# Hybrid attention layer: the split of the FFN's weights moved ahead, two scratch copies in parts, sixteen-fold queries and keys stored by residue

## The chip, the cores and the metric

One core of a Trainium2 chip runs the whole layer. The metric is the device time of one execution in microseconds (us).

## What is computed

The reference is one transformer layer in float32 on 2048 tokens of width 1024. `z = rmsnorm(x) @ w_in` gives the queries, keys and values of three mixers: sparse attention (compressed, selected and windowed keys), dilated attention with folds 1, 4 and 16, and sliding-window attention with sinks. Their outputs go through `w_out`, a norm and a residual. Then a convolutional GLU feed-forward (FFN) follows with its own norm and residual. The part that the change touches in the attention is this:

```python
for p, (w, r) in enumerate(((128, 1), (512, 4), (2048, 16))):
    def fold(a):
        return a.reshape(n, T // r, r, H, hd).transpose(0, 2, 1, 3, 4).reshape(n * r, T // r, H, hd)
    o, lse = banded_attention(fold(q[:, :, p])[:, :, :, None], fold(k[:, :, p]), fold(v[:, :, p]), w // r, ...)
```

With r = 16 a head falls into 16 independent sequences, one for each residue of the token number modulo 16, with 128 tokens each. A query tile of 128 tokens sees the 128 keys of its own residue.

## The kernel before, in words

The kernel runs five stages, one after another: `project`, `compress`, `attend`, `mix_out`, `ffn`. Between two stages all engines meet at a barrier, at which each engine first drains its own work. Products of float32 matrices are made in three passes from a rounded high part and a low part (high = value rounded to the matmul's type, low = value minus high).

**project.** `z` is made transposed, in 33 blocks j of 128 rows, with all 2048 tokens as columns in four chunks n of 512. For each block, 4 x 8 x 3 matmuls of 128x512 run (L493). Banks 4 to 7 and 0 to 3 of PSUM take turns, so TensorE starts chunk n of block j when the low part of chunk n of block j-2 has been taken. Around it:

- ScalarE rounds the weight block j+1 (`round_w`, L253) once block j-1 is through, and copies each finished chunk from PSUM to `st_hi` (L294).
- GpSimd (POOL) makes the low part of the weight block (`split_w`, L305).
- VectorE makes the low part of each chunk in `st_lo` (L411).
- SyncE issues the stores of `st_hi` and `st_lo` to the scratch tensors `z_hi`, `z_lo` in HBM, in a queue of program order, and the loads of raw weights.

POOL has a second job in this stage. It splits the FFN's weights, 33 pieces of 1 MB (`split_v`, L320 to L325): it waits for piece j, rounds it, issues the store of the high part to `f_hi`, makes the low part, issues the store to `f_lo`, and issues the load of piece j+1 (L312). Before all of it, POOL issues two copies from HBM to HBM of 4 MB each: `w1` to `w1_copy` (read by `compress`) and `w_out` to `wo_copy` (read at the end of `attend`), L337 and L338. The order is written out by hand:

```python
            load_v(0)
            pool.dma_start(w1_copy, w1).then_inc(w1_moved, 16)
            pool.dma_start(wo_copy, w_out).then_inc(wo_moved, 16)
            for j in range(NZ):
                if j >= 1 and j + 2 < NZ:
                    split_w(j + 2)
                split_v(j)
```

At the end of the stage POOL waits until all its stores have landed (L345 and the two lines before it), then drains.

**compress.** It reads the window inputs (`x_raw`, which lie in `h_hi`) and the weights (`w_raw`, which lie in `h_lo`). ScalarE makes the high parts (L623, L626), VectorE the low parts (L650, L654), then TensorE starts (L601). The second half of the weights is loaded by the first instruction of SyncE in this stage (L67).

**attend.** 36 units of 16 query tiles run in a fixed order: first k0, b0, b1, k1, b2, b3 ... k5, b10, b11, then six c units, then the w and s units. k is the compressed attention, b the dilated one; b8 to b11 are the four sixteen-fold heads. For each tile, TensorE makes the scores in two matmuls, queries x high keys (L1174) and queries x low keys (L1175); VectorE adds the bias table `near` and takes the maximum (L1361); ScalarE takes the exponential (L1282); TensorE turns the weights (L1186) and multiplies them with the values (L1211), then turns the output (L1222). Queries and keys of a head are loaded whole, 64 rows of 2048 tokens, from `z_hi` and `z_lo`. For fold 16, TensorE reads them with a step of 16 elements. SyncE's queue loads for the unit after next as soon as the running unit's scores are through: first queries, then keys, then the `near` table (L1008), later values (L1001).

In the tile names of the trace, `low` is the buffer that holds queries and half of the keys.

Of the kernel before, what the change touches and what calls it, by code (L numbers as in the profile page):

```python
# [6 lines left out]
F32 = mybir.dt.float32  # L7
# [3 lines left out]
ALU = mybir.AluOpType  # L11
AX = mybir.AxisListType

P = 128
# [39 lines left out]
V0 = 20  # L54

# [14 lines left out]
def project(nc, x, g_pre, ident, w_z, w_ffn, pos_t, z_hi, z_lo, z_pair, v_heads, gates, f_hi, f_lo, w1, w1_copy, w_out, wo_copy, wo_moved,  # L70
# [4 lines left out]
    with ExitStack() as ctx:  # L75
# [66 lines left out]

        def turned_through(j, n):

            return 4 * (j - V0) + (4 if fold_of(j) == NT else n + 1)
# [17 lines left out]
        def _(sp):  # L163
# [32 lines left out]
            for j in range(2, NZ):  # L196
# [4 lines left out]
                if j == NZ - 1:  # L201
                    for n in range(4):
                        sp.wait_ge(stored[n], stores_through(j - 1))
                    sp.wait_ge(w1_moved, 16)
                    sp.wait_ge(last_row, 2)
                    load_windows(sp, z_pair, x_raw, x2_in, 0)
                    load_first(sp, w1_copy, w1_raw, w1_in, 0)
                    load_windows(sp, z_pair, x_raw, x2_in, 1)
                for n in range(4):
# [7 lines left out]
                    sp.wait_ge(zlo_done, lowered_through(j, n))  # L217
# [15 lines left out]
        def _(act):  # L233
# [43 lines left out]
            for j in range(2, NZ):  # L277
                if j + 1 < NZ:
                    round_w(j + 1)
                for n in range(4):  # L280
                    if is_value(j - 1):

                        act.wait_ge(v_turned, turned_through(j - 1, n))
                    elif j >= 1:

                        act.wait_ge(stored[n], stores_through(j - 1))
# [3 lines left out]
                    if is_plain(j):  # L290
# [6 lines left out]
        def _(pool):  # L297
# [33 lines left out]

            split_w(0)
# [4 lines left out]
            pool.dma_start(w1_copy, w1).then_inc(w1_moved, 16)  # L337
            pool.dma_start(wo_copy, w_out).then_inc(wo_moved, 16)  # L338
            for j in range(NZ):
                if j >= 1 and j + 2 < NZ:  # L340
                    split_w(j + 2)
                split_v(j)
# [5 lines left out]
        def _(dve):  # L348
# [40 lines left out]
            for j in [*range(2, V0 + NV), NZ - 1]:  # L389
                for n in range(4):  # L390
                    if j >= 1:

                        dve.wait_ge(stored[n], stores_through(j - 1))
                    bank = banks[:, 4 * (j % 2) + n, :]
# [13 lines left out]
                    else:  # L408

                        dve.wait_ge(zhi_done, 4 * j + n + 1)  # L410
                        dve.tensor_tensor(st_lo[:, n, 0:512], bank, st_hi[:, n, :].bitcast(F32),  # L411
                                          ALU.subtract).then_inc(zlo_done, 1)
# [350 lines left out]
def attend(nc, ident, z_hi, z_lo, v_heads, gates, bias_b, bias_c, bias_s, bias_w, own_block, sinks, cmp_bias, pick_bias,  # L763
# [112 lines left out]
    with ExitStack() as ctx:  # L876
# [105 lines left out]
        def _(sp):  # L982
# [60 lines left out]
            for u in range(NU):  # L1043
# [21 lines left out]
                if u == NU - 2:  # L1065
                    sp.wait_ge(wo_moved, 16)
# [72 lines left out]
        def _(pe):  # L1139
# [3 lines left out]
            def scores(n, only):  # L1143
# [14 lines left out]
                query = q2[:, qs, :].rearrange(tok, r=unit.fold, j=P)[:, res, b, :]  # L1158
                upper = query
                if unit.kind == "k":  # L1160
                    hi, lo, start = kc_hi[:, unit.h // R, :], kc_lo[:, unit.h // R, :], 0
                else:
                    hi = k_hi[ks].rearrange("p (l r) -> p r l", r=unit.fold)[:, res, :]
                    lo = k_lo[ks].rearrange("p (l r) -> p r l", r=unit.fold)[:, res, :]
                if unit.chosen:
# [969 lines left out]
```

## Time and profile before

| | |
|---|---|
| runs | 3593.09, 3597.2, 3601.05 us; median 3597.2 us |
| profiled execution | 3595.68 us, its span 3593.9 us |
| TensorE (PE) busy | 3413.3 us, 95% of the span |
| VectorE (DVE) busy | 1412.2 us, 39% |
| ScalarE (ACT) busy | 1164.7 us, 32% |
| GpSimd (POOL) busy | 512.1 us, 14% |

`project` takes 0 to about 825 us of the span, `compress` to 862 us, the k, b and c units of `attend` to about 1276 us; the rest is the other attention units, the mix and the FFN. In the rows, a matmul's time overlaps the next one's: the step from start to start is what one costs, the duration is longer. "PE x [7.0 <-POOL y]" means that PE was idle for 7.0 us before x, and that y of POOL ended the wait. The windows view gives the busy time in each stretch by engine, the granted clock of TensorE as a share of 2.4 GHz, and the busy share of the 16 DMA engines.

### The profile page before, as it was taken

What the parts mean: (1) busy time and instruction counts of PE and PEld (TensorE: products, weight loads), DVE (VectorE), ACT (ScalarE), POOL (GpSimd) and SP (SyncE); (2) the same over time, 40 slices, a digit from 0 to 9 for tenths busy, and PEclk for the clock granted to TensorE, in tenths of its full rate; (3) what the DMA queues carried; (4) which work ended last, traced back from release to release, by engine and by line L of the source; (5) the groups of instructions that cost most, each with busy time, mean ns of one, the idle gap of its engine ahead of it and who ended that gap; (6) DMA issues with size and microseconds to landing.
All of it is one profiled execution on the core that took longest, in us unless ns stands there. A gap on an engine that the chain in (4) does not pass through costs nothing. (4 is left out here: it accounts for less than half of the span.)

```text
span 3593.9 us, 45309 instructions
## 1 busy us (share of the span) xinstructions
PE 3413.3 (95%) x16530; PEld 2720.9 (76%) x16530; DVE 1412.2 (39%) x3874; ACT 1164.7 (32%) x1980; POOL 512.1 (14%) x409
## 2 busy tenths in 40 slices
PE   8999999995898999999989969999999999999997
PEld 6788888875787876666657858887888788878886
DVE  5111101104666776666654434412541154115421
ACT  5111111114655765455433323301331133104310
POOL 1454444441000012221010000000000000000000
PEclk9999999997999999999989989999999999999999
DMA  6987765566968732332127665566556655665553
GB/s 200 324 289 258 258 224 176 203 228 178 218 166 200 170 93 59 96 94 55 51 77 234 199 218 193 193 234 233 192 196 234 228 196 197 234 216 206 196 191 117
DMA packets 297668, 676.17 MB, mean 188 GB/s; under 512 B 98704, under 2 KB 154512, under 8 KB 283408
## 3 DMA queue, kind: packets, MB, share of 16 engines
q1 hardware_dynamic: 265616, 517.93, 45.1%
q0 software_dynamic: 31840, 155.40, 12.1%
q8 instruction: 135, 2.21, 0.3%
q14 instruction: 77, 0.63, 0.1%
HBM read 496.06 MB, written 185.57 MB: 190 GB/s over the span
## 5 line engine op out<-in xcount | busy, mean ns | idle before, releaser
L1855 PE MATMUL f_banks<-low,f_w_hi 128*128 128x512 f32 x2816 | 871.3, 390 | 27.1 <-DMA f_w_lo<-f_lo 19.8
L1855 PEld LDWEIGHTS f_banks<-low,f_w_hi 128*128 128x128 f32 x2816 | 529.8, 188 | 140.4 <-issue 25.4
L1855 PE MATMUL f_banks<-low,f_w_lo 128*128 128x512 f32 x1408 | 548.8, 390 | 0.0
L1211 PE MATMUL a_ot_ps<-a_turned_w,a_vs 128*65 128x256 f32 (+3 forms) x1452 | 448.7, 421 | 1.1 <-issue 1.1
L493 PE MATMUL z_banks<-h_hi,z_w_hi 128*128 128x512 f32 x972 | 388.3, 399 | 7.0 <-POOL z_w_lo L305 7.0
L493 PE MATMUL z_banks<-h_lo,z_w_hi 128*128 128x512 f32 x972 | 385.3, 396 | 0.0
L493 PE MATMUL z_banks<-h_hi,z_w_lo 128*128 128x512 f32 x972 | 385.2, 396 | 0.0
L1855 PEld LDWEIGHTS f_banks<-low,f_w_lo 128*128 128x128 f32 x1408 | 265.0, 188 | 54.5
L1282 ACT ACTIVATE w_small<-w_small,a_negm 128x128 f32<-128x128 f32 (+3 forms) x510 | 249.4, 519 | 173.4 <-DVE a_negm L1361 108.3
L1875 PE MATMUL f_banks<-f_w_hi,f_g_hi 128*128 128x512 f32 x704 | 278.4, 396 | 0.0
L1875 PE MATMUL f_banks<-f_w_hi,f_g_lo 128*128 128x512 f32 x704 | 278.4, 396 | 0.0
L1875 PE MATMUL f_banks<-f_w_lo,f_g_hi 128*128 128x512 f32 x704 | 278.4, 395 | 0.0
L294 ACT ACTIVATE st_hi<-z_banks 128x512 fp32r<-128x512 f32 (+1 forms) x116 | 69.3, 598 | 540.8 <-PE z_banks L493 397.9
L1211 PEld LDWEIGHTS a_ot_ps<-a_turned_w,a_vs 128*65 128x65 f32 x1452 | 179.0, 139 | 82.7 <-issue 70.1
L1361 DVE CUSTOM_DVE_ANT_0 w_small<-a_s_ps,near 128x128 f32<-128x128 f32 (+2 forms) x456 | 170.5, 394 | 168.7 <-PE a_s_ps L1175 139.6
L493 PEld LDWEIGHTS z_banks<-h_hi,z_w_hi 128*128 128x128 f32 x972 | 183.5, 189 | 50.1 <-POOL z_w_lo L305 7.4
L493 PEld LDWEIGHTS z_banks<-h_lo,z_w_hi 128*128 128x128 f32 x972 | 183.2, 188 | 44.4
L493 PEld LDWEIGHTS z_banks<-h_hi,z_w_lo 128*128 128x128 f32 x972 | 183.3, 189 | 42.7
L1959 DVE SCALAR_TENSOR_TENSOR f_y<-f_banks,vk,f_gp 128x1024 f32<-128x1024 f32 x16 | 20.5, 1284 | 494.7 <-POOL vk L1808 494.2
L411 DVE TENSOR_TENSOR st_lo<-z_banks,st_hi 128x512 fp32r<-128x512 f32 x76 | 52.6, 692 | 406.2 <-ACT st_hi L294 406.2
L1186 PE MATMUL a_t_ps<-a_idt,w_small 128*128 128x128 f32 x1092 | 212.1, 277 | 0.0
L1268 ACT ACTIVATE a_turned_w<-a_t_ps 128x512 f32<-128x512 f32 (+3 forms) x255 | 138.7, 549 | 198.9 <-PE a_t_ps L1186 198.0
(212 smaller groups left out, 5302.3 us busy)
## 6 DMA issues: line engine op xcount, KB each, us to landing
f_w_hi<-f_hi SPq DMA_DIRECT2D x264, 512.0 KB, 3.5
f_w_lo<-f_lo SPq DMA_DIRECT2D x264, 512.0 KB, 4.5
z_xs<-in_w_ffn POOLq DMA_DIRECT2D x33, 1024.0 KB, 8.6
f_hi<-z_v_hi POOLq DMA_DIRECT2D x33, 1024.0 KB, 4.9
f_lo<-z_xs POOLq DMA_DIRECT2D x33, 1024.0 KB, 6.4
low<-z_hi SPq DMA_DIRECT2D x48, 512.0 KB, 7.7
z_hi<-st_hi SPq DMA_DIRECT2D x84, 256.0 KB, 4.5
z_lo<-st_lo SPq DMA_DIRECT2D x84, 256.0 KB, 5.1
```

What stands on the lines that cost most here:

```text
L294: act.activation(out.bitcast(F32) if is_value(j) else out, bank, ACT.Copy).then_inc(zhi_done, 1)
L411: dve.tensor_tensor(st_lo[:, n, 0:512], bank, st_hi[:, n, :].bitcast(F32), ALU.subtract).then_inc(zlo_done, 1)
L493: last = pe.matmul(banks[:, 4 * k + n, :], w[:, k, c, :], h[:, c, tok], start=(c == 0 and q == 0), stop=(c == DC - 1 and q == 2))
L1186: ins = pe.transpose(t_ps[:, b % TB, i, :], weights(n)[:, x * P:(x + 1) * P], idt[:])
L1211: last = pe.matmul(ot_ps[0:out_width(g), at:at + count * P], values, rows, start=(x == 0), stop=(x == len(blocks) - 1), skip_group_check=True)
L1268: ins = eng.activation(out, src, ACT.Copy) if e == 0 else eng.tensor_copy(out, src)
L1282: act.activation(weights(n), weights(n), ACT.Exp, bias=negm[:, n % 32:n % 32 + 1], scale=-1.0)\
L1361: dve.tensor_tensor_reduce(weights(n)[:, a:z], s_ps[:, c % SB, 0:z - a], table[:, at + a:at + z], -0.125, floor, ALU.add, ALU.min, low).th ...
L1855: last = pe.matmul(banks[:, bank, :], w[:, s % RING, c * P:(c + 1) * P], h[:, c, :], start=(c == 0 and x == 0), stop=(c == DC - 1 and x == 2))
L1875: last = pe.matmul(banks[:, 2 * t + n, :], g[:, d, tok], w[:, s % RING, cols], start=(d == 0 and x == 0), stop=(d == NF - 1 and x == 2))
L1959: dve.scalar_tensor_tensor(out=y[:], in0=banks[:, 2 * t:2 * t + 2, :].rearrange("p b n -> p (b n)"), scalar=rstd[:, t:t + 1], in1=gp[:], o ...
```

## The change

1. **The FFN split.** Its loop starts at j = 1, with `split_w(3)` ahead of `split_v(0)`, and at j = 4, 8 and 12 it does two pieces. So the last piece is done at j = 30, with the last `split_w`.
2. **The copies.** `w1` and `w_out` are moved in 16 parts of 256 KB each, one of either after the split at j = 6 to 21.
3. **By residue.** For the blocks 7, 8 (queries b8 to b11) and 18, 19 (their keys), the copies from PSUM to `st_hi` and `st_lo` put the 128 tokens of each residue next to each other. A chunk of 512 tokens then goes to all four slots of the buffer, so ScalarE and VectorE wait for all four stores of the block before, and SyncE stores a chunk only after all four have been lowered. In `attend`, queries and keys of fold 16 are read as 128 neighbouring columns.

```diff
+RESIDUE_BLOCKS = (7, 8, 18, 19)
+TWICE = (4, 8, 12)
+MOVES = tuple(range(6, 22))
...
+        def by_residue(bank):
+
+            return bank.rearrange("p (l m a) -> p m a l", m=4, a=4)
+
+        def residues(tile, n):
+
+            return tile[:, :, 0:512].rearrange("p m (a l) -> p m a l", a=4)[:, :, :, n * P // 4:(n + 1) * P // 4]
...
-                    sp.wait_ge(w1_moved, 16)
+                    sp.wait_ge(w1_moved, 16 * len(MOVES))
...
-                    sp.wait_ge(zlo_done, lowered_through(j, n))
+                    sp.wait_ge(zlo_done, lowered_through(j, 3 if j in RESIDUE_BLOCKS else n))
...
+                    elif j in RESIDUE_BLOCKS and n == 0:
+                        for m in range(4):
+                            act.wait_ge(stored[m], stores_through(j - 1))
...
-                    if is_plain(j):
+                    if j in RESIDUE_BLOCKS:
+                        act.activation(residues(st_hi, n), by_residue(bank), ACT.Copy).then_inc(zhi_done, 1)
+                    elif is_plain(j):
...
+            def move(i):
+
+                m, c = divmod(i, len(MOVES) // 2)
+                rows = slice(c * (CMP * HD * 2 // len(MOVES)), (c + 1) * (CMP * HD * 2 // len(MOVES)))
+                pool.dma_start(w1_copy[m, rows], w1[m, rows]).then_inc(w1_moved, 16)
+                rows = slice(i * (D // len(MOVES)), (i + 1) * (D // len(MOVES)))
+                pool.dma_start(wo_copy[rows], w_out[rows]).then_inc(wo_moved, 16)
...
-            pool.dma_start(w1_copy, w1).then_inc(w1_moved, 16)
-            pool.dma_start(wo_copy, w_out).then_inc(wo_moved, 16)
-            for j in range(NZ):
-                if j >= 1 and j + 2 < NZ:
+            v = 0
+            for j in range(1, NZ):
+                if j + 2 < NZ:
                     split_w(j + 2)
-                split_v(j)
+                for _ in range(2 if j in TWICE else 1):
+                    if v < NZ:
+                        split_v(v)
+                        v += 1
+                if j in MOVES:
+                    move(MOVES.index(j))
...
+                    if j in RESIDUE_BLOCKS and n == 0:
+                        for m in range(1, 4):
+                            dve.wait_ge(stored[m], stores_through(j - 1))
...
-                        dve.tensor_tensor(st_lo[:, n, 0:512], bank, st_hi[:, n, :].bitcast(F32),
-                                          ALU.subtract).then_inc(zlo_done, 1)
+                        low, high = st_lo[:, n, 0:512], st_hi[:, n, :].bitcast(F32)
+                        if j in RESIDUE_BLOCKS:
+                            low, high, bank = residues(st_lo, n), residues(st_hi.bitcast(F32), n), by_residue(bank)
+                        dve.tensor_tensor(low, bank, high, ALU.subtract).then_inc(zlo_done, 1)
...
-                    sp.wait_ge(wo_moved, 16)
+                    sp.wait_ge(wo_moved, 16 * len(MOVES))
...
+                if unit.fold == NT:
+                    query = q2[:, qs, res * P:(res + 1) * P]
...
+                    if unit.fold == NT:
+                        hi, lo = (k[:, res * P:(res + 1) * P] for k in (k_hi[ks], k_lo[ks]))
```

The queue of POOL at the start of the FFN split, before (z_w_lo is the low part of a weight block, z_v_hi and z_xs the two parts of an FFN piece):

```order
L305 TENSOR_TENSOR z_w_lo<-z_w_raw,z_w_hi 128x1024 x3
L312 DMA z_xs<-in_w_ffn 128x2048
L337 DMA w_copy<-in_w 64x16384
L338 DMA wo_copy<-in_w_out 64x16384
L320 TENSOR_SCALAR z_v_hi<-z_xs 128x2048
L322 DMA f_hi<-z_v_hi 128x2x1024
L323 TENSOR_TENSOR z_xs<-z_xs,z_v_hi 128x2048
L325 DMA f_lo<-z_xs 128x2x1024
L312 DMA z_xs<-in_w_ffn 128x2048
L305 TENSOR_TENSOR z_w_lo<-z_w_raw,z_w_hi 128x1024
```

The same place of POOL's queue now:

```order
L321 TENSOR_TENSOR z_w_lo<-z_w_raw,z_w_hi 128x1024 x3
L328 DMA z_xs<-in_w_ffn 128x2048
L321 TENSOR_TENSOR z_w_lo<-z_w_raw,z_w_hi 128x1024
L336 TENSOR_SCALAR z_v_hi<-z_xs 128x2048
L338 DMA f_hi<-z_v_hi 128x2x1024
L339 TENSOR_TENSOR z_xs<-z_xs,z_v_hi 128x2048
L341 DMA f_lo<-z_xs 128x2x1024
L328 DMA z_xs<-in_w_ffn 128x2048
L321 TENSOR_TENSOR z_w_lo<-z_w_raw,z_w_hi 128x1024
```

The two large copies are gone from here, and weight block 3 is lowered ahead of the first FFN piece.

The end of POOL's queue in `project`, before, from the last weight block on (L75 is the barrier, L580 is the next stage):

```order
L305 TENSOR_TENSOR z_w_lo<-z_w_raw,z_w_hi 128x1024
L320 TENSOR_SCALAR z_v_hi<-z_xs 128x2048
L322 DMA f_hi<-z_v_hi 128x2x1024
L323 TENSOR_TENSOR z_xs<-z_xs,z_v_hi 128x2048
L325 DMA f_lo<-z_xs 128x2x1024
L312 DMA z_xs<-in_w_ffn 128x2048
...
L323 TENSOR_TENSOR z_xs<-z_xs,z_v_hi 128x2048
L325 DMA f_lo<-z_xs 128x2x1024
L75 UNCONDITIONAL_BRANCH
```

The same place now (L78 is the barrier):

```order
L321 TENSOR_TENSOR z_w_lo<-z_w_raw,z_w_hi 128x1024
L336 TENSOR_SCALAR z_v_hi<-z_xs 128x2048
L338 DMA f_hi<-z_v_hi 128x2x1024
L339 TENSOR_TENSOR z_xs<-z_xs,z_v_hi 128x2048
L341 DMA f_lo<-z_xs 128x2x1024
L78 UNCONDITIONAL_BRANCH
```

Before, three pieces of the FFN came after the last weight block, now one. The two-piece rounds stand between weight blocks 6 and 7, 10 and 11, 14 and 15.

## Rows read from the trace of the kernel before

**Rows 1.** Who TensorE waited for, 0 to 1250 us: in total, times, longest.
```profile
PE c_hid L601 <- DVE h_lo L654: 29.0, 1, 29.0
PE z_banks L493 <- POOL z_w_lo L305: 7.0, 1, 7.0
```

**Rows 2.** Timeline of POOL, 78 to 135 us: start, duration, engine, line, operation.
```profile
81.56 0.54 POOL L337 DMA_DIRECT2D w_copy<-in_w  x1
...
95.25 0.57 POOL L312 DMA_DIRECT2D z_xs<-in_w_ffn  x1
...
122.60 1.91 POOL L320 TENSOR_SCALAR z_v_hi<-z_xs 128x2048 fp32r<-128x2048 f32 x1 [24.36 <-DMA z_xs<-in_w_ffn]
```

**Rows 3.** Windows behind that wait: stretch, length, busy PE PEld DVE ACT POOL, PEclk, DMA share.
```profile
134.20:139.50 5.30, 5.30 (x13) 4.14 (x14) 0.00 (x0) 0.00 (x0) 0.00 (x0) 0.50 1.01 373
139.50:150.00 10.50, 10.50 (x46) 8.46 (x45) 1.38 (x2) 1.20 (x2) 7.04 (x3) 1.00 0.58 227
```

**Rows 4.** Timeline of POOL, one later round of the FFN split.
```profile
272.99 2.40 POOL L305 TENSOR_TENSOR z_w_lo<-z_w_raw,z_w_hi 128x1024 fp32r<-128x1024 f32 x1 [10.78 <-ACT z_w_hi L253]
...
284.05 0.57 POOL L312 DMA_DIRECT2D z_xs<-in_w_ffn  x1
295.39 2.40 POOL L305 TENSOR_TENSOR z_w_lo<-z_w_raw,z_w_hi 128x1024 fp32r<-128x1024 f32 x1 [10.78 <-ACT z_w_hi L253]
```

**Rows 5.** Timelines of POOL, SyncE's queue and PE around the end of `project`.
```profile
805.33 1.89 POOL L320 TENSOR_SCALAR z_v_hi<-z_xs 128x2048 fp32r<-128x2048 f32 x1 [11.18 <-DMA z_xs<-in_w_ffn]
...
813.11 0.75 POOL L325 DMA_DIRECT2D f_lo<-z_xs  x1 [0.30 <-POOL z_xs L323]
825.37 0.31 POOL L580 MEMSET kc_hi<- 128x256 f32 x1 [11.51 <-POOLq L75]
...
806.38 0.43 SPq L230 DMA_DIRECT2D z_lo<-st_lo  x1
...
833.16 0.56 PE L601 MATMUL c_hid<-c_x_hi,h_hi 128*128 128x260 f32 x1 [29.05 <-DVE h_lo L654]
```

**Rows 6.** Timelines of DVE and POOL around the next barrier.
```profile
861.51 0.29 DVE L675 COPY vk<-c_vc_ps 127x128 f32<-127x128 f32 x1 [0.17 <-PE c_vc_ps L614]
...
862.60 1.80 POOL L1086 MEMSET k_lo<- 64x2048 f32 x1 [36.31 <-POOLq L518]
```

**Rows 7.** The instruction group of ScalarE that reads with a step of eight elements.
```profile
L623 ACT ACTIVATE c_x_hi<-h_hi 128x1024 fp32r<-128x1024 f32 x4 | 8.1, 2080 | 0.0
```

**Rows 8.** SyncE's two loads of `w1_copy` (L67), its line's view.
```profile
DMA to landing us min/median/max: 8.6/13.0/17.4
```

**Rows 9.** Timeline of PE, scores of unit k0, then of unit b8.
```profile
880.68 0.27 PE L1174 MATMUL a_s_ps<-kc_hi,low 128*128 128x128 f32 x1
880.79 0.28 PE L1175 MATMUL a_s_ps<-kc_lo,low 128*128 128x128 f32 x1
...
1090.24 0.39 PE L1174 MATMUL a_s_ps<-k_hi,low 128*128 128x128 f32 x1
1090.46 0.39 PE L1175 MATMUL a_s_ps<-k_lo,low 128*128 128x128 f32 x1
```

**Rows 10.** Windows of the units b8, b9, k5, b10, b11; columns as in rows 3.
```profile
1087.10:1102.00 14.90, 14.13 (x87) 12.59 (x86) 10.41 (x56) 9.41 (x24) 0.00 (x0) 1.00 0.69 180
1102.00:1115.20 13.20, 13.20 (x98) 13.20 (x98) 8.61 (x43) 9.83 (x23) 0.00 (x0) 1.00 0.91 200
1115.20:1127.10 11.90, 10.58 (x86) 9.03 (x85) 8.04 (x46) 7.93 (x22) 0.00 (x0) 1.00 1.05 272
1127.10:1150.30 23.20, 17.35 (x90) 14.72 (x89) 12.47 (x71) 8.69 (x23) 0.30 (x1) 0.78 0.59 147
1150.30:1166.80 16.50, 15.08 (x112) 14.35 (x110) 13.12 (x88) 10.65 (x27) 1.69 (x4) 1.00 0.97 246
```

**Rows 11.** Timeline of DVE at the first tiles of k5 and b10.
```profile
1117.09 0.29 DVE L1361 CUSTOM_DVE_ANT_0 w_small<-a_s_ps,near 128x128 f32<-128x128 f32 x1 [1.31 <-DMA near<-in_cmp_bias]
...
1132.67 0.29 DVE L1361 CUSTOM_DVE_ANT_0 w_small<-a_s_ps,near 128x128 f32<-128x128 f32 x1 [4.91 <-DMA near<-in_bias_b]
```

## The prediction

> **What bounds the kernel now.** I read the waits of TensorE first, because the page has it busy for 95% of the span: whatever does not shorten its matmuls or its waits is worth nothing. Up to the c units it has two waits that the moved work of POOL could touch [rows 1]: 29.0 us before the first product of `compress`, and 7.0 us before a product of `project`. The rest of `project` runs without a gap, one weight block of 96 matmuls every 22.4 us (start to start of the low parts in [rows 4]).
>
> The timeline of POOL explains the 7.0 us. At 81.56 it issues the 4 MB copy of `w1`, and right behind it the one of `w_out` [rows 2]. The load of FFN piece 1, issued at 95.25, meets these copies in the DMA engines, and POOL waits 24.36 us for it, until 122.60. Only after that piece's round of 9.2 us (275.39 to 284.62 in [rows 4]) comes `split_w(4)`, and TensorE, which was through at 127.2, starts block 4 at 134.2. Its clock was granted at 0.5 until 139.5, that is 1.2 instead of 2.4 GHz [rows 3]: twelve matmuls took 5.3 us, while later 45 took 10.5 us, 0.233 us each.
>
> The end of `project` explains the 29.0 us [rows 5]. TensorE ends at 833.16 - 29.05 = 804.1, SyncE issues its last store until 806.8. POOL still waits for piece 32 until 805.33, splits it, issues the store of its low part until 813.9, waits for that to land and drains. The next stage begins at 825.4. Where POOL is not last, a barrier costs 0.8 us (last work ends at 861.8, first starts at 862.6 [rows 6]).
>
> For the sixteen-fold heads I compared score matmuls of one shape. In k0, where queries and keys are neighbouring columns, starts are 0.11 us apart; in b8, with a step of 16 elements, 0.22 us [rows 9]. Then I read the units' windows [rows 10] and VectorE's waits for the bias table [rows 11], since a faster TensorE calls for the next loads earlier.
>
> **The change, term by term.**
>
> *Start of the split: -9.5 us.* `split_w(3)` comes ahead of piece 0 and the large copies are gone from here. `split_w(4)` then has only piece 0 in front of it. TensorE was through with block 3 at 127.2, so it was through with block 2 at about 104.8; ScalarE and `split_w(4)` can follow there, and piece 0, a round of 9.2 us whose load was issued at about 81, is over by then. The part is ready at about 108 and needed at 127.2. That removes 7.0 us of waiting [rows 1] and the half clock: 5.3 - 12 x 0.233 = 2.5 us [rows 3].
>
> *Two pieces in a round: 0.* The round takes 2.4 + 9.2 + 9.2 us and the wait for the second piece's load, 11.2 us at most if I take the one of [rows 5]: 32 us. The next `split_w` is asked for at 22.4 us and is 10 us late, but TensorE needs it only a block later, at 44.8. Single rounds of 11.6 us catch up at once. If that cover were gone, each of the three rounds would cost 10 us.
>
> *Copies in parts: 0.* In 16 rounds POOL issues two DMAs more, at 0.54 us each by [rows 2], or 1.1 us in a round that has 10.78 us of idle time [rows 4]. The data add 0.5 MB to a block of 22.4 us. Their readers come hundreds of us later.
>
> *Residue copies: 0.* ScalarE and VectorE now read PSUM with a step of 16 elements and write pieces of 32. No row has this. Nearest: ScalarE's reading with a step of eight took 2.08 us for 1024 elements [rows 7], so 1.0 us for a chunk of 512. A gain isn't in it, since no contiguous copy is waited for. The cover is large: a chunk comes every 22.4 / 4 = 5.6 us. The waits for all four stores hold back chunk 0 of the next copy only, on ScalarE and VectorE, and TensorE takes these banks again a whole block later. SyncE issues eight stores in one go and the next weight load 3.5 us later than now; that is needed some 20 us on.
>
> *End of `project`: -17.7 us.* Piece 32 now follows `split_w(32)`, which comes some 40 us before the end, so POOL has drained by then. SyncE is last: 806.8 + 0.8 = 807.6 in place of 825.4 [rows 5, 6]. TensorE's idle time shrinks from 29 to some 11 us; the half clock behind it stays, since it came after 7 us too [rows 3].
>
> *Inputs of `compress`: +1 us.* With 18 us less, the second half of `w1_copy` is loaded while the last stores of `z` still run. Its two loads took 8.6 and 17.4 us [rows 8]. At 8.6 it is in time; at 17.4 it costs about 5.5, since ScalarE turns to it some 12 us into the stage, after four copies of 2.08 us [rows 7] and four of about half of that. I take 1, near the short one: POOL's five transfers, which made the long one long, are gone. Bounds 0 and 5.5.
>
> *Scores of b8 to b11: -5.7 us.* Each unit has 32 such matmuls, so 32 x 0.11 = 3.5 us at most [rows 9]; the last of each pair is followed by an instruction of another kind that waits for its own weights, so I take 2.6. How much of it counts:
> - b8: TensorE is busy for 14.1 of 14.9 us, VectorE 10.4 [rows 10]. All of it, 2.6.
> - b9: TensorE is full, but behind it k5 starts with a wait of 1.31 us for its table, and b10 with one of 4.91 us [rows 11]. Both tables are last in a row of loads that is issued when b8 and b9 are through. The DMA share is 0.91 and 1.05 in b9 and k5 [rows 10]: the queue is full from the end of b8 on. A shorter b9 makes these waits longer. I take 0.3; bounds 0 and 2.6.
> - b10: it lasts 23.2 us with 17.35 of TensorE, and contains the selection of blocks on VectorE. I take 1.5; bounds 0 and 2.6.
> - b11: DMA share 0.97, and c0's table comes the same way. I take half, 1.3; bounds 0 and 2.6.
>
> Sum: -9.5 - 17.7 + 1 - 5.7 = -31.9 us, from 3595.7 for the profiled execution to 3563.8. The median of the runs lies 1.5 above that execution, so the forecast is **3565 us**.
>
> The Trainium skill, SBUF — State Buffer, "Door 1: The DMA port swizzle", says that a transfer to 64 partitions uses half of the ports and reaches 196 GB/s where it was measured at 1 MiB. Queries and keys are loaded just so, and an estimate from that page is 2.7 us for each 0.5 MiB, 13.4 us for the five ahead of a table. By that rule alone no b unit could beat the loads, b9 to b11 would give nothing, and the sum would be -28.8. The trace agrees that the table is late in k5 and b10 [rows 11], but b11 and b8 show that it isn't always.
>
> **Rivals.**
>
> *A. All of the scores' gain counts.* The loads are asked for earlier by as much as the units shorten, and the full share is not a limit but a burst. Then 10.4 instead of 5.7: 3560. Against it: the two waits in [rows 11]. Chance 0.13.
>
> *B. The loads take it all.* The waits grow by what the units lose, b8 included: 3565 + 5.7 = 3571. For it: shares near 1. Against it: 0.69 in b8. The page's rule above leads to nearly the same place, 3568. Chance 0.14.
>
> *C. The wait at the end of `project` is filled by another.* `compress` starts early, but its inputs are late by the upper bound or more, and the half clock lasts longer. 17.7 shrinks to about 9: 3574. Chance 0.09.
>
> *D. The early wait stays,* because something else holds block 4: 3574.5. Against it: nothing else in POOL's queue is left there. Chance 0.03.
>
> *E. Slower than before: POOL's issues become its work.* If a part of a copy costs POOL far more than the whole copy did, `split_w` falls behind in 16 rounds and TensorE waits in each. It decides at (22.4 - 11.6) / 2 = 5.4 us for one issue; at 7 us the rounds cost 16 x (11.6 + 14 - 22.4) = 51 us, so 3616. Against it: 0.54 us for 4 MB [rows 2]. Chance 0.02.
>
> *F. The change doesn't do what it says for the scores:* the 0.11 us have another cause than the step (the pairs share a shape, but not the tiles that they read), and only the two waits go: 3571, as B, and counted there.
>
> **How the numbers follow.** The forecast has a chance of 0.59: 3565, on its own between 3560 and 3570. To it come A 0.13, B and F 0.14, C 0.09, D 0.03, E 0.02. From 3557 (A, with `compress` not delayed and a run's scatter of 3 us) to 3576 (C and D) all but E and a tenth is in. A difference of 0.2%, 7 us, is about what a measurement of this kernel can tell from none; every case but E lies more than 20 us below 3597. For what I have not seen I leave 0.02 to no difference and 0.02 in all to slower, so faster has 0.96.
>
> **What the profile would show.** No wait of TensorE for L305's successor near 134, and block 4 at full clock. POOL idle before the barrier, SyncE the last to arrive, the next stage about 1 us after SyncE's last store. In `compress`, ScalarE's second half without a wait for `w1_copy`. Starts of 0.11 us in the scores of b8 to b11, longer waits for `near` in k5, b10 not shorter by more than 2 us. The prediction is wrong if TensorE waits in blocks 6 to 21, if a residue copy takes over 5 us, or if attention gains 10 us or nothing.

## The result, and the profile after

The changed kernel takes 3564.2 us (median of 4 runs, 3559.7 to 3572.1) against 3599.1 us (4 runs, 3593.1 to 3601.8). The ratio is 0.9908, interval 0.9884 to 0.9931. The forecast was 3565, with a range of 3557 to 3576. The profiled execution has a span of 3557.9 us, 36.0 less than before.

Who TensorE waited for from 0 to 1250 us, as in [rows 1] (L634 is the old L601; all lines after the change have moved):

```profile
PE a_s_ps L1211 <- DVE a_negm L1398: 16.8, 25, 2.5
PE z_banks L459 <- DVE z_xs L391: 16.6, 4, 10.1
PE a_s_ps L1211 <- DMA low<-z_lo: 15.5, 2, 9.1
PE a_on_ps L1259 <- ACT a_ot L1327: 12.0, 22, 1.9
PE c_hid L634 <- DVE h_lo L687: 11.2, 1, 11.2
```

The wait for POOL's low part of a weight block is gone from the list, and the one before `compress` is 11.2 in place of 29.0 us. The others were there before: the first two with 16.6 and 16.9 us, nearly the same sums, the wait for `z_lo` with 13.7 and the one for `a_ot` with 8.4 us, so these two have grown by 1.8 and 3.6 us.

**The start of the split.** The timeline of POOL, to be held against [rows 2]:

```profile
94.58 0.56 POOL L328 DMA_DIRECT2D z_xs<-in_w_ffn  x1
105.80 2.39 POOL L321 TENSOR_TENSOR z_w_lo<-z_w_raw,z_w_hi 128x1024 fp32r<-128x1024 f32 x1 [10.65 <-ACT z_w_hi L264]
108.17 1.91 POOL L336 TENSOR_SCALAR z_v_hi<-z_xs 128x2048 fp32r<-128x2048 f32 x1
```

The third row is piece 1, which began at 122.60 before. Weight block 4 is ready at 108.2 (108 was forecast). The products of `project` end at 793.8 in place of 804.1 us; 0.7 of the 10.3 us were already there when its first whole block began.

**A round with two pieces**, timeline of POOL at the end of the round of j = 4 (first row) and in the next one:

```profile
179.32 0.56 POOL L328 DMA_DIRECT2D z_xs<-in_w_ffn  x1
179.90 2.41 POOL L321 TENSOR_TENSOR z_w_lo<-z_w_raw,z_w_hi 128x1024 fp32r<-128x1024 f32 x1
189.05 1.91 POOL L336 TENSOR_SCALAR z_v_hi<-z_xs 128x2048 fp32r<-128x2048 f32 x1 [6.75 <-DMA z_xs<-in_w_ffn]
```

Rounds began at 105.80, 128.20, 150.60; the next should have begun at 173.0 and begins 7 us late, at 179.90. Between 90 and 790 us TensorE never has more than 0.33 us from one start to the next, so the cover held here and in the other two. POOL did not catch up at once: the single pieces after it waited 6.75 and 5.93 us for their loads, and only the third round after, at 217.8, is on time again. After the rounds of j = 8 and 12 it was the same (8.9 and 7.8 us late, then 4.6 and 4.2, then on time).

**The end of `project`**, timelines of POOL, of SyncE's queue and of PE, as in [rows 5]:

```profile
765.93 0.75 POOL L341 DMA_DIRECT2D f_lo<-z_xs  x1 [0.30 <-POOL z_xs L339]
797.18 0.30 POOL L613 MEMSET kc_hi<- 128x256 f32 x1 [30.51 <-POOLq L78]
...
795.70 0.43 SPq L241 DMA_DIRECT2D z_lo<-st_lo  x1
797.50 0.37 SPq L70 DMA_DIRECT2D h_lo<-w_copy  x1
...
804.97 0.56 PE L634 MATMUL c_hid<-c_x_hi,h_hi 128*128 128x260 f32 x1 [11.15 <-DVE h_lo L687]
```

POOL now idles for 30.51 us until the next stage, which starts 1.0 us after SyncE's last store. Before, POOL's last store (issued at 813.11) landed at 821.6, its drain took 2.7 us more, and the stage began at 825.37. From the last product of `project` to the first of `compress` it is 11.2 us, 17.9 less than before.

**The residue copies** on ScalarE, its line's view:

```profile
L305 ACT ACTIVATE st_hi<-z_banks x16: 591/597/600, 199.4 to 485.0; 128x512 fp32r<-128x512 f32 x16
...
  DMA z_lo<-st_lo: 23.1, 2
```

They take 0.597 us, as the contiguous ones. The 23.1 us are two waits for all four stores (13.7 and 9.4 us), in the second block of each pair, 8 and 19; VectorE's copies came later by them, and TensorE had no gap there.

**The scores.** Timeline of PE in b8, against the b8 of [rows 9]:

```profile
1064.03 0.28 PE L1211 MATMUL a_s_ps<-k_hi,low 128*128 128x128 f32 x1
1064.14 0.28 PE L1212 MATMUL a_s_ps<-k_lo,low 128*128 128x128 f32 x1
1064.25 0.27 PE L1211 MATMUL a_s_ps<-k_hi,low 128*128 128x128 f32 x1
```

Starts are 0.11 us apart, as in k0. The windows of b8, b9, k5, b10, b11, columns as in [rows 10]:

```profile
1057.90:1070.50 12.60, 10.77 (x86) 9.10 (x86) 9.95 (x55) 8.65 (x23) 0.00 (x0) 1.00 0.76 199
1070.50:1081.50 11.00, 10.60 (x98) 10.03 (x98) 7.76 (x42) 8.37 (x23) 0.00 (x0) 1.00 0.95 212
1081.50:1099.50 18.00, 14.92 (x86) 12.74 (x86) 8.34 (x46) 8.61 (x23) 0.00 (x0) 0.72 1.02 248
1099.50:1114.75 15.25, 11.22 (x91) 9.49 (x90) 11.79 (x70) 8.46 (x23) 0.00 (x0) 1.00 0.66 172
1114.75:1130.80 16.05, 12.57 (x112) 11.05 (x110) 13.25 (x88) 9.88 (x26) 1.98 (x4) 1.00 0.97 241
```

Lengths before were 14.9, 13.2, 11.9, 23.2 and 16.5 us: b8 and b9 gain 2.2 each, k5 gives 6.1 back, b10 gains 8.0, b11 0.5. Of the 6.1 us of k5, 2.5 are a longer wait for its table (3.79 in place of 1.31); behind it the granted clock was at half for 10.2 us, which it was nowhere in k5 before. VectorE's waits for the tables of k5 and b10, as in [rows 11], and the first load that SyncE issued when the scores of b8 were through:

```profile
1085.91 0.29 DVE L1398 CUSTOM_DVE_ANT_0 w_small<-a_s_ps,near 128x128 f32<-128x128 f32 x1 [3.79 <-DMA near<-in_cmp_bias]
...
1101.18 0.29 DVE L1398 CUSTOM_DVE_ANT_0 w_small<-a_s_ps,near 128x128 f32<-128x128 f32 x1 [0.95 <-DMA near<-in_bias_b]
...
1070.72 0.46 SPq L1018 DMA_DIRECT2D low<-z_hi  x1
```

From that load to the end of the wait in b10 it is 1101.18 - 1070.72 = 30.46 us. Before, the same load was issued here:

```profile
1102.20 0.46 SPq L985 DMA_DIRECT2D low<-z_hi  x1
```

and the wait ended at 1132.67 [rows 11]: 30.47 us. A faster b9 changed nothing in between; the loads set this stretch. That the two numbers agree to a hundredth is luck: in the other eight profiles with the table last (section 2 puts it first) it is 30.7 to 31.4 us. In it the five loads of 0.5 MB ahead of k5's table landed 2.4 to 2.9 us apart, from 1075.45 to 1085.69, and the table right behind them, at 1085.89.

### The profile page after: what moved, and what is told of

It reads as the page before. It is cut to its first block and busy times, and to the rows that moved or that the text cites. A ratio compares the mean times of both kernels' runs of the same rounds, so it can differ in the third digit from the quotient of the medians.

```text
span 3557.9 us, 45347 instructions
## 1 busy us (share of the span) xinstructions
PE 3400.4 (96%) x16530; PEld 2708.7 (76%) x16530; DVE 1411.4 (40%) x3874; ACT 1161.3 (33%) x1980; POOL 527.3 (15%) x439
## 5 line engine op out<-in xcount | busy, mean ns | idle before, releaser
L310 ACT ACTIVATE st_hi<-z_banks 128x512 fp32r<-128x512 f32 (+1 forms) x100 | 59.7, 597 | 461.3 <-PE z_banks L526 336.1
```

The costliest lines, as they stand in the source:

```text
L310: act.activation(out.bitcast(F32) if is_value(j) else out, bank, ACT.Copy).then_inc(zhi_done, 1)
```

## Experiments

All times are medians. Stretches come from one profiled execution of each kernel.

### 1. Each part by itself

The step of 16 back:

```diff
-RESIDUE_BLOCKS = (7, 8, 18, 19)
+RESIDUE_BLOCKS = ()
...
-                if unit.fold == NT:
-                    query = q2[:, qs, res * P:(res + 1) * P]
...
-                    if unit.fold == NT:
-                        hi, lo = (k[:, res * P:(res + 1) * P] for k in (k_hi[ks], k_lo[ks]))
```

> The changed kernel with its third part undone: blocks 7, 8, 18, 19 stored in token order, fold 16 read with a step of 16. Theory: the three parts are independent and the scores' part is worth 6.8 us (b8 to b11, from the traces before and after). Then the time is 3564 + 7 = 3571, the stages before the scores stay as in the changed kernel, score steps are 0.22 us again, and b10 waits 4.9 us for its table. Rival: storing by residue costs something in `project` that the scores pay back; then the scores start earlier than in the changed kernel, and the loss is below 6.8.

Measured: 3571.5 us (ratio to before 0.9922, interval 0.9898 to 0.9946). The scores start at 841.4 (841.9 in the changed kernel), so the residue copies cost nothing. b8 to b11 with k5 take 79.5 us (79.7 before, 72.9 in the changed kernel), and b10 waits 5.4 us for its table (4.9 expected).

The old order of the split:

```diff
-            v = 0
-            for j in range(1, NZ):
-                if j + 2 < NZ:
+            for j in range(NZ):
+                if j >= 1 and j + 2 < NZ:
                     split_w(j + 2)
-                for _ in range(2 if j in TWICE else 1):
...
+                split_v(j)
                 if j in MOVES:
                     move(MOVES.index(j))
```

> The changed kernel with the old loop of the FFN split (piece j in round j, piece 0 ahead of weight block 3, three pieces after the last weight block), but the copies still in 16 parts in rounds 6 to 21. Theory: the end of `project` costs 17.9 us again, because POOL is last at the barrier, and the early wait of 7.0 us stays away, since it was made by the two 4 MB copies in front of piece 1: 3564 + 18 = 3582. Rival: the early wait is made by the order (a piece of the FFN ahead of a weight block) and comes back too: 3564 + 18 + 9.6 = 3592.

Measured: 3583.3 us (0.9957, 0.9941 to 0.9973). TensorE has no gap in `project`, whose products end at 794.4; `compress` starts at 824.2, so the way between them is 29.8 us again, 18.7 more than in the changed kernel. POOL's timeline there, its wait for piece 1:

```profile
95.44 0.56 POOL L328 DMA_DIRECT2D z_xs<-in_w_ffn  x1
96.02 2.40 POOL L321 TENSOR_TENSOR z_w_lo<-z_w_raw,z_w_hi 128x1024 fp32r<-128x1024 f32 x1
104.31 1.93 POOL L336 TENSOR_SCALAR z_v_hi<-z_xs 128x2048 fp32r<-128x2048 f32 x1 [5.89 <-DMA z_xs<-in_w_ffn]
```

5.89 in place of 24.36 us, with the large copies gone and nothing else changed here.

The copies whole, in the new order:

```diff
             load_v(0)
+            pool.dma_start(w1_copy, w1).then_inc(w1_moved, 16)
+            pool.dma_start(wo_copy, w_out).then_inc(wo_moved, 16)
             v = 0
...
-                if j in MOVES:
-                    move(MOVES.index(j))
```

> The changed kernel with the two copies of 4 MB whole and at their old place, the new order of the split kept. Theory: piece 1 is late again by some 24 us, but weight block 4 is now ahead of it in POOL's queue, so TensorE waits for nothing: 3564, no difference. Rival: the copies alone make the wait, by whatever they delay (raw weights, stores of z): TensorE waits some us before 140 again and runs at half clock behind it, 3564 + 9.6 = 3574.

Measured: 3566.1 us (0.9911, 0.9877 to 0.9944), no gap of TensorE in `project`. But POOL's timeline shows that it was close:

```profile
95.47 0.56 POOL L328 DMA_DIRECT2D z_xs<-in_w_ffn  x1
120.67 2.39 POOL L321 TENSOR_TENSOR z_w_lo<-z_w_raw,z_w_hi 128x1024 fp32r<-128x1024 f32 x1 [24.63 <-ACT z_w_hi L264]
```

The copies delay the raw weights too. Block 4 is ready at 123.1 where TensorE wants it at about 126. So the early wait needed both the copies in front and a piece of the FFN ahead of the weight block; either half of the change takes it away.

The residue part alone, on the kernel before:

```diff
             load_v(0)
-            v = 0
-            for j in range(1, NZ):
-                if j + 2 < NZ:
+            pool.dma_start(w1_copy, w1).then_inc(w1_moved, 16)
+            pool.dma_start(wo_copy, w_out).then_inc(wo_moved, 16)
+            for j in range(NZ):
+                if j >= 1 and j + 2 < NZ:
                     split_w(j + 2)
...
+                split_v(j)
```

> The kernel before with the third part alone: stored by residue, read as neighbouring columns; split and copies as before. Theory: only b8 to b11 shorten, by 6.8 us in sum, and the start of the scores stays at 870: 3599 - 7 = 3592. Of it, b8 and b9 give 2.2 each, k5 takes 6 back and b10 gives 8, because the table of b10 lands 30.4 us after the end of b8's scores in either kernel. Rival: the gain depends on the earlier stages' DMA work and comes out elsewhere, under 3 or over 10 us.

Measured: 3591.2 us against 3596.3 in the same rounds (0.9984, 0.9969 to 0.9999). The early wait is there (6.9 us), and the scores start at 868.3. b8, b9, k5, b10, b11 take 13.0, 11.0, 17.8, 17.2 and 15.2, in sum 74.1: 5.5 less than before. The stretch from the first load after b8 to b10's table was 31.2 us, not 30.4, and b10 gave 6.0 us in place of 8. The parts add up: 17.9, 9.6, and 3.4 to 6.8 for the scores (b8 to b11 with k5 in the five profiles that have this code: 72.9 to 76.3, against 79.5 and 79.7 with the step) make 31 to 34, and 35.0 was measured.

### 2. What holds the shorter units back

```diff
                 sp.wait_ge(scored, through(u))
+                sp.wait_ge(biased, through(u))
+                for n, x in near_at.after.get(u, []):
+                    load_near(n, x)
                 for n, x in q_at.after.get(u, []):
                     load_q(n, x)
...
-                sp.wait_ge(biased, through(u))
-                for n, x in near_at.after.get(u, []):
-                    load_near(n, x)
```

> The changed kernel, but SyncE waits for VectorE too and then loads the `near` table of the unit after next ahead of the queries and keys. Theory: what took the gain of b9 is the place of the table behind 2.5 MB of other loads, not the bandwidth as such. Then VectorE's waits of 3.8 us in k5 and 1.0 in b10 go, k5 is at 12 us again and b10 at 14 or less, b0 and b1 shorten a little: 3564 - 8 = 3556. Rival: the DMA engines are full and the wait moves from the table to queries or keys: k5 and b10 keep their sum of 33 us, no difference, 3564.

Measured: 3557.5 us (0.9886, 0.9867 to 0.9905). All waits for `near` are gone, k5 takes 13.8 in place of 18.0 us and b10 15.7, so k5 and b10 have 29.5 us in place of 33.2. The theory was near in the sum and not in the parts: it had 12 and 14 us. The rival was half right. The DMA engines are full (a share of 1.02 in k5), and a part of the wait moved to queries: b10's first product, at 1092.68, waits 2.4 us for the low part of them, which counts into k5's 13.8 us. The waits from 1060 to 1115 us, with the table first:

```profile
PE a_s_ps L1211 <- DMA low<-z_lo: 2.4, 1, 2.4
```

and in the changed kernel, from 1057.9 to 1115 us:

```profile
DVE w_small L1398 <- DMA near<-in_cmp_bias: 3.8, 1, 3.8
DVE w_small L1398 <- DMA near<-in_bias_b: 1.4, 2, 1.0
```

b8 to b11 with k5 take 68.5 us here, below all five profiles with the table last (72.9 to 76.3), so the gain is more than their scatter, though the intervals of the two ratios overlap. Of the 4.2 us of k5, some 1.4 are the difference of the waits (3.8 and 2.4 us). With the waits for tables the half clock went too: it was granted for 10.2 us in k5 in the changed kernel, and in the five units here for 3.4 us in all, from 1105.7 to 1109.1 us, over the end of b10. So the order of the queue took most of b9's gain, partly by the wait itself and partly by the half clock behind it, and bandwidth took the rest. How much of it is the clock's isn't separated.

### 3. Which operand the step is paid for

```diff
-                if unit.fold == NT:
-                    query = q2[:, qs, res * P:(res + 1) * P]
+                step = {8: (NT, 1), 9: (1, NT), 10: (4, 4), 11: (2, 2)}.get(unit.h, (1, 1))
+                def every(buf, s):
+                    return buf[:, res * P:(res + 1) * P] if s == 1 else buf.rearrange("p (l r) -> p r l", r=s)[:, res % s, 0:P]
+                if unit.fold == NT:
+                    query = every(q2[:, qs, :], step[0])
...
-                        hi, lo = (k[:, res * P:(res + 1) * P] for k in (k_hi[ks], k_lo[ks]))
+                        hi, lo = (every(k, step[1]) for k in (k_hi[ks], k_lo[ks]))
```

> The changed kernel with other steps of reading in the four units (it reads wrong elements there, so these heads' scores are others; the output is not the layer's). b8: queries (the weights of TensorE) with a step of 16, keys neighbouring. b9: keys (the moving columns) with a step of 16, queries neighbouring. b10: both with a step of 4. b11: both with a step of 2. Theory M: the moving columns set the 0.22 us, so b9 has 0.22 and b8 0.11 from start to start. Theory W: the weights set it, so b8 has 0.22 and b9 0.11. By the page SBUF - State Buffer of the Trainium skill a step of up to 4 elements of fp32 is free, so b10 and b11 would be at 0.11; by the steps of 0.24 us that the fold 4 heads show for 256 columns, against 0.12 in fold 1, a step of 4 doubles the time, and b10 would be near 0.12 only because a matmul of 128 columns is not bound by its columns.

This kernel was run once. The line's view of L1214 (the first of each pair) in b8, b9, b10, b11, duration of min/median/max in ns:

```profile
L1214 PEld LDWEIGHTS a_s_ps<-k_hi,low x14: 291/304/313, 1060.2 to 1073.5; 128*128 128x128 f32 x14
...
L1214 PEld LDWEIGHTS a_s_ps<-low x14: 186/191/192, 1076.4 to 1085.0; 128*128 128x128 f32 x14
...
L1214 PEld LDWEIGHTS a_s_ps<-k_hi,low x11: 308/330/333, 1104.0 to 1116.4; 128*128 128x128 f32 x11
...
L1214 PEld LDWEIGHTS a_s_ps<-low x12: 193/196/198, 1126.2 to 1136.4; 128*128 128x128 f32 x12
```

Timeline of PE in b8 (queries with a step of 16), in b9 (keys with a step of 16) and in b10 (both with a step of 4):

```profile
1067.00 0.38 PE L1214 MATMUL a_s_ps<-k_hi,low 128*128 128x128 f32 x1
1067.22 0.38 PE L1215 MATMUL a_s_ps<-k_lo,low 128*128 128x128 f32 x1
...
1079.62 0.30 PE L1215 MATMUL a_s_ps<-low 128*128 128x128 f32 x1
1079.73 0.30 PE L1214 MATMUL a_s_ps<-low 128*128 128x128 f32 x1
...
1112.98 0.42 PE L1214 MATMUL a_s_ps<-k_hi,low 128*128 128x128 f32 x1
1113.22 0.42 PE L1215 MATMUL a_s_ps<-k_lo,low 128*128 128x128 f32 x1
```

Theory W holds. Queries with a step of 16 make the load of the weights 0.304 us long and the starts 0.22 apart; keys with a step of 16 leave them at 0.11. The units follow: b8 takes 14.7 us, as before the change, and b9 10.9. A step of 4 is no better than 16 (0.330 us for the load, starts 0.23 apart), a step of 2 is nearly free (0.196, starts 0.12 apart in b11). In b10 the keys had a step of 4 too, but the queries' loads alone take as long in the fold 4 heads: 0.31 to 0.33 us in b4 to b7 in the changed kernel, 0.19 where the queries lie by residue and the keys don't (section 5).

The Trainium skill, SBUF — State Buffer, in the note on cachelines in "Door 1: The DMA port swizzle", says that a line has 16 bytes and needs at least two hits for full bandwidth, and also that fp32 can be strided by 4 for free. For loads of weights the trace agrees with the first (a step of 2 puts two fp32 elements in 16 bytes, a step of 4 one) and not with the second, if that means a step of 4: 0.330 against 0.191 us. And my own guess in the expectation, that b10 would be bound by neither, was wrong, since its weights had the step as well.

### 4. Queries alone

```diff
-RESIDUE_BLOCKS = (7, 8, 18, 19)
+RESIDUE_BLOCKS = (7, 8)
...
-                    if unit.fold == NT:
-                        hi, lo = (k[:, res * P:(res + 1) * P] for k in (k_hi[ks], k_lo[ks]))
```

> The changed kernel with only the queries of fold 16 stored by residue (blocks 7, 8); their keys stay in token order and are read with a step of 16. After the run with other steps, where queries with a step gave 0.22 us and keys with a step 0.11: the gain is all in the queries, b8 to b11 as in the changed kernel, 3564. Rival: keys with a step cost something that the median of the steps did not show (their matmul lasted 0.30 in place of 0.28 us): 2 us in all, 3566.

Measured: 3567.1 us (0.9917, 0.9898 to 0.9937). b8 and b9 take 12.8 and 11.1 us (12.6 and 11.0). With keys and queries it was 3564.2 and, run again, 3562.4; their intervals overlap, so the times don't tell theory and rival apart. Nor does b8, which takes 12.6 to 13.2 us in the five profiles with one code. In b9, which takes 10.97 to 10.99 us in all five and 11.14 here, the keys' part of the change is worth about 0.15 us.

### 5. Fold 4 too

Keys and queries of fold 4 by residue, then the same with the table first, then queries alone for both folds with the table first:

```diff
-RESIDUE_BLOCKS = (7, 8, 18, 19)
+RESIDUE_BLOCKS = (5, 6, 7, 8, 16, 17, 18, 19)
+BY_FOUR = (5, 6, 16, 17)
...
+            if j in BY_FOUR:
+                return bank.rearrange("p (l a) -> p a l", a=4)
...
+            if j in BY_FOUR:
+                return tile[:, :, n * P:(n + 1) * P]
...
-                if unit.fold == NT:
-                    query = q2[:, qs, res * P:(res + 1) * P]
+                if unit.fold > 1:
+                    query = q2[:, qs, t * P:(t + 1) * P]
...
-                    if unit.fold == NT:
-                        hi, lo = (k[:, res * P:(res + 1) * P] for k in (k_hi[ks], k_lo[ks]))
+                    if unit.fold > 1:
+                        hi, lo = (k[:, res * per * P:(res + 1) * per * P] for k in (k_hi[ks], k_lo[ks]))
```

The third kernel has only the blocks of queries, 5 to 8, in `RESIDUE_BLOCKS`, and reads all keys with their step.

> The changed kernel with the fold 4 heads (b4 to b7; blocks 5, 6, 16, 17) stored by residue and read as neighbouring columns too. Theory: steps of 0.38 and 0.24 us become 0.20 and 0.12 as in fold 1, at most 4 x 16 x 0.295 = 18.9 us; b6 and b7 are full on TensorE, b4 and b5 have other waits, and a unit can't end before its loads of 12 to 14 us, so 12 of it count: 3564 - 12 = 3552. Rival: the loads take it back as they did in b9: under 5 us, 3560.

> Both: fold 4 by residue and the table first. Theory: the table first lets more of the shorter units count, so the two add or more: 3564 - 8 - 14 = 3542. Rival: bandwidth bounds the sum, and the two give no more than the better of them: 3552.

> Queries alone by residue for folds 4 and 16, and the table first. If keys with a step are free at 256 columns and a step of 4 too, b4 to b7 are as short as with keys by residue (19.2, 18.3, 15.3, 17.1 us) and the time is that of that kernel, 3555. If a step of 4 costs the moving columns at 256, b6 and b7 lie nearer to 17.7 and 19.1 us, and the time is 3560.

Measured: 3554.8 us (0.9880, 0.9862 to 0.9898), 3555.1 (0.9885, 0.9864 to 0.9907) and 3559.8 (0.9894, 0.9873 to 0.9916). The lengths in us:

| | b4 | b5 | b6 | b7 | k5 | b10 | b11 | k0 to b1 |
|---|---|---|---|---|---|---|---|---|
| changed kernel | 20.4 | 21.0 | 17.7 | 19.1 | 18.0 | 15.2 | 16.0 | 53.1 |
| fold 4 too | 19.0 | 19.4 | 15.3 | 17.1 | 17.9 | 15.9 | 15.6 | 52.2 |
| and table first | 19.2 | 18.3 | 15.3 | 17.1 | 13.7 | 17.3 | 16.6 | 55.7 |
| queries alone, table first | 18.8 | 20.4 | 17.0 | 18.7 | 13.2 | 15.3 | 16.9 | 53.7 |

Fold 4 gives 7.3 us in b4 to b7, less than the 12 expected, though more than the rival's 5. Here the keys do matter: with queries alone b6 and b7 gain only 0.7 and 0.4. The second matmul of a pair, L1217 with keys by residue and L1215 without, in the line's view of b6:

```profile
L1217 PE MATMUL a_s_ps<-k_lo,low x16: 273/282/287, 1002.8 to 1017.6; 128*128 128x256 f32 x12, 128*128 128x128 f32 x4
...
L1215 PE MATMUL a_s_ps<-k_lo,low x15: 316/432/435, 1006.2 to 1022.0; 128*128 128x256 f32 x12, 128*128 128x128 f32 x3
```

Moving columns with a step of 4 cost about 1 ns each (0.25 us from start to start for 256), neighbouring ones about half (0.12 us). At 128 columns the first would make 0.13 us, near the 0.11 us from start to start that matmuls of 128 neighbouring columns take; with a step of 16 section 3 measured 0.11 too. Why the step is hidden there no run shows.

The table first and fold 4 together should have given another 4 to 6 us and did not: 3555.1 us is no more than the better of the two gives, as the rival had it (3552). k5 gained its 4 us as before, and b10, b11 and the three first units lost them. These places differ between runs of one code as well (next section). Whether the combination costs something there or drew badly stays open.

### 6. The changed kernel again

> The changed kernel once more, to see how much of a unit's length changes from run to run. The sum from b8 to the start of c0 was 72.9 us there, and 74 to 76 in kernels with the same code in these units; the granted clock was at half in k5 alone in the first, in k5 and b10 in the others. If that is the cause, the sum lies between 73 and 77 here too and goes with the place of the half clock. The time: 3564.

Measured: 3562.4 us (0.9902, 0.9884 to 0.9919). b8 to b11 with k5 take 74.5 us. k5 has the same length (18.1), b10 has 17.1 in place of 15.2. In the first profile the clock was at half from 1086.9 to 1097.1 only, all in k5, where time was to spare: however early k5 ends, b10 waits for its table. In this one it was at half from 1087.7 to 1097.9 and once more from 1115.0 to 1118.4, over the end of b10 at 1117.3. Over the kernels with the same code in these units (five profiles) the sum is 72.9 to 76.3.

The half clock accounts for most of what b10 does. From the end of its wait for the table to b11's first score, in us, in the nine profiles with the table last and one step for all of b8 to b11:

| | of it at half clock | from the wait's end to b11 |
|---|---|---|
| step of 16: before, step back | 10.2, 10.2 | 17.6, 17.6 |
| by residue: old order, copies whole | 6.8, 6.8 | 16.1, 15.9 |
| queries by residue alone | 3.4 | 14.9 |
| by residue: residue alone, again | 2.1, 2.3 | 14.6, 14.7 |
| by residue: changed kernel, fold 4 too | 0, 0 | 13.6, 13.6 |

The windows of this stretch before and in the changed kernel:

```profile
1132.67:1150.30 17.63, 14.09 (x72) 12.28 (x73) 11.81 (x66) 7.26 (x19) 0.30 (x1) 0.71 0.47 114
...
1101.18:1114.75 13.57, 9.69 (x79) 8.20 (x77) 11.07 (x65) 6.97 (x19) 0.00 (x0) 1.00 0.61 150
```

By residue, 6.8 us at half cost 2.4 to 2.5 us, 0.35 to 0.37 each. At that price 10.2 us at half make 3.5 to 3.8 us of the 4.1 between the first row and the last. This estimate leaves 0.3 to 0.6 us to the step itself.

## Why the prediction was right

By its own terms, from the two profiled executions:

| term | forecast | measured |
|---|---|---|
| start of the split | -9.5 | -9.6, and 0.7 before it |
| two pieces in a round, copies in parts, residue copies | 0 | 0 |
| end of `project` | -17.7 | -17.9 |
| inputs of `compress` (to its last product) | +1 | -0.3 |
| scores, b8 to b11 | -5.7 | -6.8 |
| everything else | 0 | -0.7 |
| sum | -31.9 | -36.0 |

By medians the gain is 35.0 us, so 31.9 was about 3 too small. That 3564.2 then met 3565 within a microsecond is partly luck: the kernel before came out 1.9 us higher with its fourth run (3599.1 in place of 3597.2), and the forecast was built on the lower one.

- **Start of the split.** Right in size and mechanism: the copies made piece 1 late, and the order put it ahead of block 4. I took the two together; the runs of section 1 show that one would have done.
- **Two pieces, residue copies.** Both cost nothing, as forecast, but not all of the reasoning held. Single rounds did not catch up at once, since their pieces waited for loads too; it took two rounds more. And the 1.0 us for a residue copy, taken from a read of SBUF with a step of eight [rows 7], was 0.597.
- **End of `project`.** Right: POOL was last only because of pieces 31 and 32. With the old order the 18 us came back alone.
- **Inputs of `compress`.** The loads of `w1_copy` took 10.6 and 11.3 us, between the two bounds, and the second landed half a microsecond before ScalarE turned to it. The 1 us was not spent. The 0.3 us gained are gone by the first score: from the first product of `compress` to it there are 37.0 us in both kernels.
- **Scores.** The sum was near, its parts were not. For b8 I took 2.6 and it gave 2.2 (1.7 to 2.2 over the five profiles with this code). For b9 I took 0.3 on the ground that the tables of k5 and b10 would hold; they did, and b9, k5 and the wait in b10 together gained nothing. The term that was mis-sized is b10: I took 1.5 and put all of it on the step. From the end of its wait to the end of the unit it went from 17.6 to 13.6 us, 4.1 less, and by the table in section 6 most of that is the clock, which the term left out. Before, the half clock fell twice into b10, with a mean of 0.78 [rows 10]; after, it fell into k5, behind the longer wait there, where time was to spare. Where it falls differs from run to run: over the five profiles with this code this gain is 1.6 to 4.1 us, and the sum for the scores -3.4 to -6.8; the first profile has the largest. b11 gave 0.5 in place of 1.3. And one sign was wrong: b10 was to be not over 2 us shorter, and it was 8.0 shorter, since 4.0 us of its wait moved into k5.
- **The cause of 0.22 us.** I put it down to the step of queries and keys alike. It is the queries, which TensorE loads as weights; at 128 columns the keys' half of the change does next to nothing. The forecast did not depend on it.
- **The rivals.** A (the whole gain of the scores) did not happen, because of the waits it was weighed against. B was right for b9 only. C, D and E did not occur: an issue of a part took POOL 0.5 us. F is out by the steps of 0.11 us in b8 after the change and of 0.22 in section 3, where only the queries' step was put back.

The prediction took from the Trainium skill (SBUF — State Buffer, "Door 1: The DMA port swizzle") an estimate of 2.7 us for each load of 0.5 MB to 64 partitions, by which b9 to b11 would have given nothing. The trace agrees on the pace: five such loads landed 2.4 to 2.9 us apart. It agrees on b9, which gave nothing. b10 and b11 gave something, b10 mostly by the clock.

## What to carry to other kernels

At a barrier, look for the engine that arrives last and ask whether its last work belongs there; moving side work ahead by two rounds, where its engine had half of each round free, was worth 18 us. A large copy whose reader is far away should not stand in front of loads that are needed now, and short of moving it, what waits for the slow load can be put behind what does not (either half alone took the early wait away here). When a unit gets shorter, look at what is queued for the next ones: a small table behind 2.5 MB of other loads took a gain back, and moving it to the front shortened the five units by 4.4 us and the median by 5 to 7.

## What was not expected of the hardware

- Loads of weights (128x128, fp32 read as fp32r) took 0.19 us with neighbouring columns, 0.196 with a step of 2, 0.33 with 4 and 0.30 to 0.31 with 16. Moving columns with a step cost about 1 ns in place of 0.5 ns each, which shows at 256 columns and not at 128.
- Copies from PSUM with a step of 16 elements took 0.597 us for 512 elements on ScalarE, the same as contiguous ones. Reading SBUF with a step of eight took 2.08 us for 1024 elements [rows 7], twice the 1.05 us of neighbouring ones.
- In the two profiles of the changed kernel most of the difference lies in the FFN. From the last score to the end of the span it took 1769.1 us in the first and 1778.9 in the second, while the last score came only 1.4 us later. Most of these 9.8 us are waits of TensorE for ScalarE's scaling of a finished bank. The waits of TensorE from 1789 us on in the first and from 1791 us on in the second:

```profile
PE f_banks L1892 <- ACT f_acc L1938: 1.5, 2, 1.0
...
PE f_banks L1892 <- ACT f_acc L1938: 9.1, 3, 5.6
```

The clock was at half about two of these waits (2838.7 to 2842.1 and 3207.4 to 3214.2 us) and not there in the first profile. What makes ScalarE late in one run and not in another stays open.
